# Modulation from unsplit weights, four column groups at a time, in a two-block transformer kernel

## What is computed

```python
mod = silu(c) @ w_mod + b_mod            # c: (1, 1024), w_mod: (1024, 6144)
modc = silu(c_ctx) @ w_mod + b_mod
sh1, sc1, g1, sh2, sc2, g2 = split(mod, 6)
csh1, csc1, ... = split(modc, 6)
h = rms(x) * (1 + sc1) + sh1             # 512 tokens
hc = rms(xc) * (1 + csc1) + csh1         # 256 context tokens
P, Pc = project(h), project(hc)          # dense, then conv, head norms, rope
# gated delta rule, attention, Fourier mixing, MLP; then the second block
```

## Time and profile before

| | |
|---|---|
| median of 3 runs | 3386.84 us (3376.26 to 3394.01) |
| the profiled execution | 3384.86 us, span of the core 3383.0 us |
| mean granted clock of PE | 0.968 of full |
| busy: PE | 3196.6 us (94%) |
| busy: DVE, ACT, POOL | 1835.8 (54%), 1156.2 (34%), 145.5 (4%) |
| chain that ended last, by engine | PE 85%, DVE 4%, issue 3%, ACT 1% |
| matmuls L1270 (modulation) | 384, 64.0 us busy |
| splits L1611 (ACT), L1886 (DVE), L2408 (POOL) | 539, 507 and 32 |
| transfers | 288.19 MB, mean 85 GB/s |

### The profile page before, as it was taken

One profiled execution on the slowest core, in us unless ns is written; L12 is line 12 of the kernel. 1 busy time (PEld: TensorE's weight loads), 2 busy tenths in 40 slices (PEclk: granted clock), 3 DMA queues, 4 the chain that ended last, 5 costly groups with the idle time before them and its releaser, 6 DMA issues.

```text
span 3383.0 us, 42671 instructions
## 1 busy us (share of the span) xinstructions
PE 3196.6 (94%) x17636; PEld 2530.3 (75%) x17636; DVE 1835.8 (54%) x2569; ACT 1156.2 (34%) x1614; POOL 145.5 (4%) x126
## 2 busy tenths in 40 slices
PE   5877898889999999999999999999999999999997
PEld 2665684468888888876678888888887767888886
DVE  6445565454435544477865434564344877653446
ACT  4433112533324322333443222442223244432233
POOL 0223340000000000000000000000000000000000
PEclk7888996999999999999999999999999999999999
DMA  5223000013232232221122332233222212223222
GB/s 182 88 90 117 25 3 30 1 69 99 94 100 97 93 99 98 94 90 63 57 87 100 100 100 89 94 111 96 97 88 96 88 50 75 101 94 100 94 90 72
DMA packets 81936, 288.19 MB, mean 85 GB/s; under 512 B 9552, under 2 KB 11344, under 8 KB 81360
## 3 DMA queue, kind: packets, MB, share of 16 engines
q1 hardware_dynamic: 81744, 285.46, 25.1%
HBM read 283.33 MB, written 2.10 MB: 84 GB/s over the span
## 4 chain that ended last, share of the span: by engine, by line
PE 85%; DVE 4%; issue 3%; ACT 1%; POOL 0%; DVEq 0%; ACTq 0%; POOLq 0%
PE PS L1253 74%; PE PS L1331 2%; PE PS L1557 1%; PE PS L1501 1%; PE PS L1521 1%; PE PS L1559 1%; PE PS L1578 1%; PE PS L1509 1%; ACT SPL L1611 1%; PE PS L1567 1%; DVE SM L2184 0%; PE PS L1540 0%; PE PS L1291 0%; PE PS L1502 0%; DVE GC L2352 0%
## 5 line engine op out<-in xcount | busy, mean ns | idle before, releaser
L1253 PE MATMUL PS<-HS,SPL 128*128 128x512 f32 (+2 forms) x7752 | 1803.8, 393 | 19.1 <-DVE HS L1936 10.8
L1253 PEld LDWEIGHTS PS<-HS,SPL 128*128 128x128 f32 (+2 forms) x7752 | 1452.0, 188 | 342.2 <-issue 29.1
L1886 DVE TENSOR_TENSOR SPL<-RAW,SPL 128x1024 fp32r<-128x1024 f32 (+2 forms) x507 | 614.4, 1215 | 767.7 <-ACT SPL L1611 763.9
L1611 ACT ACTIVATE SPL<-RAW 128x1024 fp32r<-128x1024 f32 (+1 forms) x539 | 551.6, 1031 | 902.9 <-PE PS L1253 862.8
L1253 PE MATMUL PS<-FF,SPL 128*128 128x512 f32 x2880 | 654.6, 389 | 0.0
L1253 PEld LDWEIGHTS PS<-FF,SPL 128*128 128x128 f32 x2880 | 540.6, 188 | 112.2
L2269 DVE SCALAR_TENSOR_TENSOR CA<-AP__149,CW,CA 128x512 f32<-128x512 f32 x240 | 180.0, 750 | 6.2
L1782 ACT ACTIVATE FF<-TMP 128x512 fp32r<-128x512 f32 x88 | 55.7, 633 | 235.4 <-DVE TMP L2239 235.4
L1776 ACT ACTIVATE SA<-SA 128x512 f32<-128x512 f32 x88 | 55.5, 633 | 191.7 <-DVE SA L2229 191.7
L2229 DVE TENSOR_TENSOR SA<-PS,R 128x512 f32<-128x512 f32 x88 | 60.5, 692 | 98.8 <-PE PS L1253 98.5
L2184 DVE TENSOR_REDUCE SM<-PS 128x1 f32<-128x768 f32 (+2 forms) x96 | 61.8, 643 | 85.3 <-PE PS L1502 48.9
(11 more groups left out here) (291 smaller groups left out, 2461.8 us busy)
## 6 DMA issues: line engine op xcount, KB each, us to landing
RAW<-in_w_ff_in SPq DMA_DIRECT2D x176, 512.0 KB, 3.6
RAW<-in_w_in SPq DMA_DIRECT2D x88, 512.0 KB, 3.6
RAW<-in_w_ff_out SPq DMA_DIRECT2D x80, 512.0 KB, 3.5
RAW<-in_w_ff SPq DMA_DIRECT2D x64, 512.0 KB, 3.6
RAW<-in_w_mod SPq DMA_DIRECT2D x48, 512.0 KB, 4.6
RAW<-in_w_out SPq DMA_DIRECT2D x24, 512.0 KB, 3.6
RAW<-in_w_ple_gate SPq DMA_DIRECT2D x16, 512.0 KB, 3.6
RAW<-in_w_ff_out SPq DMA_DIRECT2D x16, 256.0 KB, 2.7
```

The lines of the kernel that those rows point to most:

```text
L1253: m = pe.matmul(o, w[x][:, k, rows], r.T[:, r.k0 + k, y, 0:r.cols], start=r.start and k == 0 and (x, y) == (0, 0), stop=r.stop and k == r. ...
L1611: a.activation(SPL[:, s, 0, 0:n], RAW[:, s, 0:n], AF.Copy).then_inc(w_hi, 1)
L1886: v.tensor_tensor(SPL[:, s, 1, 0:n], RAW[:, s, 0:n], SPL[:, s, 0, 0:n], ALU.subtract).then_inc(w_lo, 1)
```

## The change

Modulation pieces are no longer split (`whole`). silu(c) is written once as float32 into C32, 32 columns a k-tile of which two are not zero (GpSimd zeroes it first). The matmul for k-tile k of a piece writes PSUM partitions 32k to 32k+31, so the four k-tiles use four column groups of the array; each is a four-pass float32 matmul with the unsplit weights as the moving operand. All 128 partitions of the bank are copied to MR, which has four buffers in turn, and a column of `sel` (1 where the partition is 0 or 1 modulo 32) sums the four groups when the rows become columns. In the stage with rate 2 the columns are planned when three more groups of dense matmuls have passed. SP refills the slot of a modulation piece when PE has used it (`passed`, planned after the piece's matmuls); the splits of dense pieces stay where they were, three pieces ahead.

```diff
-    def piece(src, nk, ncol, pool=False):
+    def piece(src, nk, ncol, whole=False):
         p = Rec()
-        p.i, p.src, p.nk, p.ncol, p.pool, p.lo, p.used = len(pieces), src, nk, ncol, pool, None, None
+        p.i, p.src, p.nk, p.ncol, p.whole, p.lo, p.used = len(pieces), src, nk, ncol, whole, None, None
+        p.landed = (ld[p.i % 4], 16 * (p.i // 4 + 1))
         pieces.append(p)
         return p
...
     def mod(j):
         u = single()
         for a in range(0, 8, 4):
             r = Rec()
-            r.p, r.use, r.k0, r.opens = piece(W["w_mod"][j][:, a:a + 4, :], 4, 256, j >= 8), u, a, True
+            r.p, r.use, r.k0, r.opens = piece(W["w_mod"][j][:, a:a + 4, :], 4, 256, True), u, a, True
...
-        r.use, r.after, r.j = u, rows[0], j
+        r.use, r.after, r.j = u, rows[j % 4], j
...
-        soon.append(columns)
+        if rate[0] > 1:
+            later.append([3, columns])
+        else:
+            soon.append(columns)
...
+    while later:
+        passed()
     catch_up()
...
             while ahead < min(r.p.i + 4, len(pieces)):
                 p = pieces[ahead]
-                p.lo = count(w_lo_pool if p.pool else w_lo)
-                STEPS.append(("split", p))
                 ahead += 1
+                if not p.whole:
+                    p.hi, p.lo = count(w_hi), count(w_lo)
+                    STEPS.append(("split", p))
         STEPS.append((kind, r))
+        if kind == "mod_mm":
+            STEPS.append(("passed", r.p))
...
+        def passed(p):
+            if p.i + 4 < len(pieces):
+                sp.wait_ge(*p.used)
+                fetch(pieces[p.i + 4])
...
         def mod_mm(r):
-            w = parts(r.p)
             if r.p.i == 0:
-                pe.wait_ge(s_c4, 2)
-            pe.wait_ge(*r.p.lo)
+                pe.wait_ge(s_c, 1)
+            pe.wait_ge(*r.p.landed)
             if r.k0 == 0:
                 opened(r.use)
             for k in range(4):
-                for x in (0, 1):
-                    m = pe.matmul(PS[0:4, r.use.b, 0:256], C4[:, r.k0 + k, :], w[x][:, k, :],
-                                  start=r.k0 + k == 0 and x == 0, stop=r.k0 + k == 7 and x == 1)
+                m = pe.matmul(PS[32 * k:32 * k + 32, r.use.b, 0:256], C32[:, r.k0 + k, :],
+                              RAW[:, r.p.i % 4, 256 * k:256 * k + 256], start=r.k0 == 0, stop=r.k0 == 4)
...
-                m = pe.matmul(PS[:, r.use.b, 2 * i:2 * i + 2], TMP[0:4, 2, 128 * i:128 * i + 128], SEL[:, :],
+                m = pe.matmul(PS[:, r.use.b, 2 * i:2 * i + 2], MR[:, r.j % 4, 128 * i:128 * i + 128], vec("sel", 0, 2),
                               start=True, stop=True)
...
-            v.tensor_copy(TMP[0:4, 2, 0:256], PS[0:4, r.use.b, 0:256]).then_inc(free[r.use.b], 1)
+            v.tensor_copy(MR[:, r.j % 4, :], PS[:, r.use.b, 0:256]).then_inc(free[r.use.b], 1)
```

More of the change, by code:

```diff
@@ L316, in build @@
     m_bf = [(landed[n], 16) for n in ("idb", "causal", "madd")]
-    emit("c_parts", None)
+    emit("c_column", None)
     mod_mark = {}
-    rows = [None]
+    rows = [None] * 4
     def mod(j):
@@ L338, in columns @@
             q.use, q.row, q.j = single(), u, j
-            rows[0] = q.use.mark
+            rows[j % 4] = q.use.mark
             emit("mod_col", q)
             mod_mark[j] = give(q.use)
-        soon.append(columns)
-    first_sum = [True]
+        if rate[0] > 1:
+            later.append([3, columns])
+        else:
+            soon.append(columns)
     def stats_add(x, acc, mark, first, slots=(0, 1, 2)):
@@ L596, in build @@
         mod(next(nxt))
+    while later:
+        passed()
     catch_up()
-    phase = [hs_last, kv[-1], ev_marks["z", 1], bd["v", 1], *bd["cv"], bd["t", 1], mod_mark[23], rows[0]]
+    phase = [hs_last, kv[-1], ev_marks["z", 1], bd["v", 1], *bd["cv"], bd["t", 1], mod_mark[23], rows[3]]
     m_msk = load("msk", MSK[:, :, :, :], D["c_levels"], *phase)
@@ L1226, in final @@
             sp.dma_start(out_rows[:, r.j, :], XT[:, r.j, :]).then_inc(s_out, 16)
-        does = {"split": split, "load": load, "final": final}
+        does = {"split": split, "passed": passed, "load": load, "final": final}
         for kind, r in STEPS:
@@ L1596, in _, with c_column @@
         own.n = 0
-        def c_parts(r):
+        def c_column(r):
             a.wait_ge(*m_vec)
[L1600 to L1604, removed]
+            a.wait_ge(s_czero, 1)
+            a.activation(C32[:, :, 0:2], vec("c", 0, 16).rearrange("p (k c) -> p k c", c=2), AF.Silu).then_inc(s_c, 1)
         def split(p):
             s, n = p.i % 4, p.nk * p.ncol
-            a.wait_ge(ld[s], 16 * (p.i // 4 + 1))
+            a.wait_ge(*p.landed)
             if p.i >= 4:
@@ L1853, in ple_out @@
             a.activation(r.T[:, r.j, 0, :], XT[:, r.j, :], AF.Copy, scale=vec(r.gname, r.j)).then_inc(s_hhi, 1)
-        does = {"c_parts": c_parts, "split": split, "square": square, "rms": rms, "modulate": modulate,
+        does = {"c_column": c_column, "split": split, "square": square, "rms": rms, "modulate": modulate,
                 "gate_act": gate_act, "gate_exp": gate_exp, "to_sbuf": to_sbuf, "conv3_2": conv3_2,
@@ L2378, in final @@
                                    op0=ALU.mult, op1=ALU.mult).then_inc(s_fin, 1)
-        does = {"c_parts": c_parts, "split": split, "mod_row": mod_row, "mod_col": mod_col, "square": square,
+        does = {"c_column": halves_of_one, "split": split, "mod_row": mod_row, "mod_col": mod_col, "square": square,
                 "rms": rms, "gain": gain, "modulate": modulate, "modulate_lo": modulate_lo, "gates": gates,
@@ L2401, in _, with c_zero @@
         own.n = 0
-        def split(p):
-            if not p.pool:
-                return
-            s, n = p.i % 4, p.nk * p.ncol
-            g.wait_ge(w_hi, p.i + 1)
-            g.tensor_tensor(SPL[:, s, 1, 0:n], RAW[:, s, 0:n], SPL[:, s, 0, 0:n], ALU.subtract).then_inc(w_lo_pool, 1)
+        def c_zero(r):
+            g.memset(C32[:, :, :], 0.0).then_inc(s_czero, 1)
         def zeros(r):
@@ L2445, in conv_pad @@
             g.memset(AP_[:, :, 0:30], 0.0).then_inc(s_apad, 1)
-        does = {"split": split, "zeros": zeros, "inv_l": inv_l, "inv_a": inv_a, "scan_0": scan_0,
+        does = {"c_column": c_zero, "zeros": zeros, "inv_l": inv_l, "inv_a": inv_a, "scan_0": scan_0,
                 "scan_a": scan_a, "conv_pad": conv_pad}
@@ L2564 @@
          "dt": gate_cols(x["dt_bias"][0]), "alog": gate_cols(x["a_log"][0]),
-         "on": np.broadcast_to(x["o_norm_g"][0], (128, 64)), "fin": col(x["g_final_2"])}
+         "on": np.broadcast_to(x["o_norm_g"][0], (128, 64)), "fin": col(x["g_final_2"]),
+         "sel": (np.arange(128)[:, None] % 32 == np.arange(2)[None, :]).astype(f)}
     for l in range(2):
```

22 lines of the change are left out of this document (7 added, 15 removed).

## The result

Median 3413.11 us (3410.32 to 3415.18, 5 runs) against 3384.62 us for the kernel before on the same chip (3376.26 to 3394.01, 5 runs): ratio 1.0083, 95% interval 1.0062 to 1.0104. The forecast was 3389 us with a range of 3366 to 3405; it lies too low and outside its range. The profiled execution's span is 3411.6 us against 3383.0, 28.6 us longer.

What follows compares the result with a forecast made beforehand. Up to 347 us, TensorE's 42.0 us of waits for VectorE's row copies were the largest thing aimed at. 8.6 us lost in the pairs less 4.3 gained in the front, on 3384.86, gave 3389 us, range 3366 to 3405.

Steps and rivals of the forecast that it cites:

- The weights' way: In each pair, dense pieces are fetched only when slots free, two trips in series: splits at T + 6.2 and T + 14.1.
- d1: First of two dense pieces after a pair's four modulation pieces; forecast to be split at T + 6.2 us.
- T: Moment at which PE has used the first modulation piece of a pair; the forecast's times in a pair count from it.
- d2: Second of two dense pieces after a pair's four modulation pieces; forecast to be split at T + 14.1 us.
- The first matmul that waits for DVE: End point of each pair's working, counted from T; pairs sum to 12.6 us lost, 8.6 after the modulation matmuls' gain.
- The front: Stretch up to the first dense matmul at 67.51 us: gain 4.3 us, DVE's last row behind splits of pieces 17 and 18.
- g8: Last of eight pairs of modulation chunks: DVE's last modulation column 17.9 us after T instead of 13.0, loss 4.9 us.
- R2: Rival in the front: DVE not held by splits of 17 and 18; gain 18 us instead of 4.3, 3375 us; chance 0.15.
- R3: Rival: row-copy waits go, nothing replaces them if d1 is split at T; 86.7 us gained, 3298; chance 0.08, whole or part.
- R4: Rival at the opening of d1: dense group waits for the second row's bank; 4 us a pair, 3409 us; chance 0.12.
- R5: Rival in modulation matmuls: four groups in single file at half clock, 3.5 us a piece; 3411 or more; chance 0.08.
- R6: Rival in modulation matmuls: weight loads stand in the open, 5.8 us, 3395 us; chance 0.05.

Runs made afterwards that it cites:

- e1_near: Changed kernel with splits of dense pieces planned one piece ahead instead of three until the last modulation piece is opened: 3350.06 us, 0.9893.
- e9_order: Changed kernel with only SP's queue altered: refills issued in the order of the pieces, splits still three ahead: 3372.41 us, 0.9961.
- e5_dose: Changed kernel with an extra unread 512 KB transfer ahead of each dense piece's transfer that refills a modulation piece's slot: 3443.99 us, 1.0188.
- e10_ringdose: x_ring with splits one piece ahead instead of three, plus the extra transfer of e5_dose ahead of each dense fetch: 3333.20 us, 0.9847.
- x_ring: Changed kernel with dense pieces landing in two buffers of their own, so fetched long before T; splits three ahead: 3337.83 us, 0.9857.
- e4_last: Changed kernel with splits planned one piece ahead in the last pair, g8, alone: 3403.35 us, 1.0043.
- e3_rows: Kernel before the change with only four row buffers in turn and columns three dense groups later: 3379.35 us, 0.9978.
- e2_soon: Changed kernel with the columns one tick after their row, as before the change: 3415.10 us, 1.0098.
- e7_control: Kernel before the change with the edit of e1_near, splits one piece ahead instead of three: 3397.89 us, 1.0043.

## Why the prediction was wrong, point by point

- *The weights' way.* Right in mechanism and size: d1's split at T + 5.9 (forecast 6.2), d2's at T + 13.5 (14.1), in g3; the spacing of the two is 7.6 (7.9). e1_near, e9_order, e5_dose with e10_ringdose and x_ring show that it is the cause.
- *The first matmul that waits for DVE*: g1 19.2 us after T (forecast 19.2), g2 19.3 (19.9), g3 21.5 (22.5), g5 19.3 (19.7); d1 of g7 at T + 7.9 (7.7). In g1 the agreement is in part luck: ACT has the square for L1330 ready at 124.40, and PE comes to it only at 125.11, because d1 had waited for DVE to empty its bank. PE's time for a piece, 0.53 us, lies in the forecast's 0.45 to 0.9.
- *The front.* -3.8 (forecast -4.3); splits of 17 and 18 done at 50.6 and 58.3 (48.5 and 56.2); L1298 for xc at 59.06 (57.1). The total is nearer than its working: the first dense matmul comes 2.2 us earlier (65.32 against 67.51), not 4.3. The other 1.6 are won between it and g1, which the forecast had unchanged: 40.1 us at a granted clock of 1.00 instead of 41.8 at 0.80. That is luck.
- *The step that failed first: g8.* I took it for a pair like the others and counted two trips. Behind the last pair the plan also puts a third split ahead of m4's row, a third trip in series, so DVE's last modulation column ended at T + 23.2 instead of 17.9: +5.3 us on the term. e4_last takes the last two trips out of the way of the rows: g8 is 15.2 us shorter there.
- *The second: I ended each pair's working at the first matmul that waits.* The rest of the pair was taken as unchanged. It is not: in g6 24 records of a dense matmul after the stall take 7.51 us, where before 36 took 8.77 (5.85 for 24), and the next pair's m1 waits 2.0 us for a bank that ACT empties (FT, above). g6 has 3.7 us of this kind, and g3 4.0, of which 1.4 are such a bank (KT). Without g8's 5.3, 10.2 of the pairs' 15.5 us above the forecast (24.1 against 8.6) remain for it: g6 3.7, g3 3.0, g5 1.7, the others 1.8.
- *The third: the late columns were put at no cost.* The forecast counted the turns of the banks only for a dense group that takes a row's bank (R4). It had no term for the shift of all later turns, which costs 3.9 us of waits within the pairs (part of the second step) and 4.3 in the attention; the end of the working at 347 us left no place for the latter. Another 4.0 us after 368 us are the clock, for 2.6, and a rest. The 8.3 us after 368 and g8's 5.3 make 13.6 of the profile's miss of 24.3 us; 10.2 are the second step's, and 0.5 the front's.
- *R2* fell: DVE was held by the splits of 17 and 18. *R3's* condition held in x_ring: with the waits gone and d1 split in time the gain is 75 us against the changed kernel and 48.5 (1.4%) against the old one, but its price of 86.7 us was too high by 38: most of it is that e3_rows shows the 42.0 us of waits to be worth 11 in the part and 7 at the end. *R4*: L1264 waited for L1891 twice, 5.1 us in all, in g1 and g2, where the forecast had found g1 alone. In g2 the wait lies under the next one (3.1 us for ACT); in g1 PE comes 0.7 us after ACT's result, so it is covered but for that. *R5* fell by measurement: with four groups 0.53 us a piece, in single file 1.8.
- *R6* fell too: 224 records with four column groups take 14.8 us, 0.066 each, less than the 0.109 us of one weight load, so the loads lie under matmuls and under each other. By the Trainium skill (TensorE: Matmul & The Clock Gate, Part 3, The mechanism) that takes different row groups; these all use all rows, and the measurement decides.

## What to carry to other kernels

A buffer that is refilled only when its last reader is done makes the next consumer pay a whole trip; before fusing a staging copy away, ask who refills the slot and give the pieces that follow a place to land ahead of time. Where a queue holds "wait for piece n's conversion" ahead of "fetch piece n + 1", trips run in series, and every step that an in-order engine has behind such a conversion is late with it. A long wait at one matmul (here 36 us, and 73.6 in e2_soon) may be worth far less than it lasts when the same engine is what the next matmuls wait for. Where buffers or banks are given out in turn, a step that is moved shifts every later turn: compare the waits of stages that the change doesn't touch, too, before giving a difference there to the clock.

## What the runs showed of the hardware that was not expected

Four column groups of four-pass float32 matmuls run 3.4 times as fast as one (50.4 / 14.8 us for 224 records), and PE's weight loads too shrink from 23.7 to 6.3 us of busy time though each keeps its 110 ns. The same 118 matmul records, with the same banks, took 51.7 us in the kernel before at a granted clock of 0.57 and 47.0 in e7_control at 0.68: on this kernel such a phase is worth as much as a small change.
